# A two-layer diffusion trunk: the first layer's two projections change places, and every projection takes its jobs one token tile at a time

## The reference

```python
h_l = modulate(x, norm1_g[layer], sh1, sc1)      # rmsnorm(x, g) * (1 + scale) + shift
# even layer: one projection h @ ev_w_in, 2304 columns, cut into
#   qa 512, ka 512, va 512 (differential attention), qb 512, kb 128, vb 128 (windowed attention)
qa = rmsnorm(qa.reshape(B, N, DIFF_HEADS, 2, HEAD_DIM), q_g)     # ka, qb, kb likewise
if rope:                                          # latent tokens only
    qa, ka, qb, kb = [rope_2d(t, cos, sin) for t in (qa, ka, qb, kb)]
# odd layer: h @ od_w_in = q_a 512, kv_a 256, k_r 32, nq 512, nk 512, nv 512
```

## Time and profile before

| | us |
|---|---|
| median of 3 runs (3949.11 to 3957.30) | 3950.14 |
| the profiled execution's own time | 3954.3 |
| its span | 3952.5 |
| PE busy in it | 3590.1 (91%) |
| VectorE busy | 2003.9 (51%) |
| ScalarE busy | 1296.8 (33%) |
| GpSimd busy | 171.2 (4%) |

### The profile page before, as it was taken

How to read it: one execution, slowest core, us unless ns; L and a number is a source line. 1 busy time by engine, 2 the same in 40 slices (tenths; PEclk the granted TensorE clock), 3 DMA queues, 4 the chain that set the end, 5 groups by cost and what they waited for, 6 DMA issues and landing times. The chain is left out here.

```text
span 3952.5 us, 47916 instructions
## 1 busy us (share of the span) xinstructions
PE 3590.1 (91%) x17932; PEld 2879.1 (73%) x17932; DVE 2003.9 (51%) x2906; ACT 1296.8 (33%) x2312; POOL 171.2 (4%) x186
## 2 busy tenths in 40 slices
PE   8687889696899999999997979699799889999999
PEld 2476766586788888888885858577577688888887
DVE  2474355586664444434454445588654373333333
ACT  2353234465441111111114535466433351111111
POOL 0210020000120000000001100000000020000000
PEclk9898989898999999999998989799899999999999
DMA  8345464441332222212213344422444331111112
GB/s 309 102 150 174 127 134 97 98 107 59 94 89 65 65 69 60 60 54 68 68 43 133 133 160 136 120 67 58 95 90 106 97 104 46 45 49 48 50 53 69
DMA packets 439684, 370.72 MB, mean 94 GB/s; under 512 B 103509, under 2 KB 382437, under 8 KB 434405
## 3 DMA queue, kind: packets, MB, share of 16 engines
q1 hardware_dynamic: 439525, 368.61, 32.8%
HBM read 280.86 MB, written 87.69 MB: 93 GB/s over the span
## 5 line engine op out<-in xcount | busy, mean ns | idle before, releaser
L2036 DVE SCALAR_TENSOR_TENSOR xT<-ps,mods,xT 128x1024 f32<-128x1024 f32 x192 | 189.4, 1014 | 424.0 <-PE ps L2250 424.0
L2250 PE MATMUL ps<-e_gh,e_w2h 128*128 128x512 f32 x1280 | 356.8, 377 | 5.9 <-DVE e_w2l L2492 3.6
L2250 PE MATMUL ps<-e_gl,e_w2h 128*128 128x512 f32 x1280 | 352.8, 373 | 0.0
L2250 PE MATMUL ps<-e_gh,e_w2l 128*128 128x512 f32 x1280 | 352.3, 373 | 0.0
L2542 DVE TENSOR_TENSOR e_plain<-e_plain 128x1280 f32<-128x1280 f32 (+1 forms) x64 | 86.9, 1358 | 479.6 <-ACT e_plain L2407 479.6
L2250 PE MATMUL ps<-e_hl,e_w1h 128*128 128x512 f32 (+1 forms) x1200 | 327.2, 370 | 0.0
L2250 PE MATMUL ps<-e_hh,e_w1l 128*128 128x512 f32 (+1 forms) x1200 | 327.2, 370 | 0.0
L2250 PE MATMUL ps<-e_hh,e_w1h 128*128 128x512 f32 (+1 forms) x1200 | 327.1, 370 | 0.0
L2407 ACT ACTIVATE e_plain<-ps 128x1280 f32<-128x1280 f32 (+1 forms) x64 | 72.7, 1135 | 758.5 <-PE ps L2250 757.0
L2250 PEld LDWEIGHTS ps<-e_gh,e_w2h 128*128 128x128 f32 x1280 | 225.0, 190 | 55.3 <-DVE e_gl L2546 8.0
L2250 PEld LDWEIGHTS ps<-e_gh,e_w2l 128*128 128x128 f32 x1280 | 226.3, 190 | 43.5
(11 more groups left out here) (349 smaller groups left out, 7458.8 us busy)
## 6 DMA issues: line engine op xcount, KB each, us to landing
e_raw<-in_mlp_w SPq DMA_DIRECT2D x64, 512.0 KB, 4.2
e_raw<-in_mlp_w SPq DMA_DIRECT2D x128, 256.0 KB, 3.0
aw<-in_ada_w SPq DMA_DIRECT2D x12, 2048.0 KB, 8.2
e_raw<-in_w_out SPq DMA_DIRECT2D x48, 512.0 KB, 3.8
rstd<-in_ada_w SPq DMA_DIRECT2D x64, 384.0 KB, 3.4
qkC<-pc_stage SPq DMA_DIRECT2D x72, 192.0 KB, 2.7
hT<-pa_hb SPq DMA_DIRECT2D x10, 1024.0 KB, 5.4
qkA<-pa_stage SPq DMA_DIRECT2D x20, 512.0 KB, 3.2
```

The lines of the kernel that those rows point to most:

```text
L2036: ins = k.nc.vector.scalar_tensor_tensor(out=x, in0=ps, scalar=k.mods[:, layer, gate, bass.ds(n, 1), w], in1=x, op0=ALU.mult, op1=ALU.add)
L2250: mm = pe.matmul(k.ps[:, SB * (e % 2) + b, 0:n], w[:, e % 2, f], m[:, f, c0:c0 + n], start=(f == 0 and x == 0), stop=(f == nf - 1 and x == 2))
```

## The change

The list of jobs goes through all units of a tile before the next tile, from tile 0 on; before, tiles 0 and 1 went through each unit together. With that `split_at` is the first job of the tile, always, and is dropped. And `pb` is called first, with `keeps_h=True`, and `pa` second, with `keeps_h=False`.

```diff
-    jobs = [(t, j) for j in range(U) for t in range(2)] + [(t, j) for t in range(2, NT) for j in range(U) if t < LT or not units[j].latents]
+    jobs = [(t, j) for t in range(NT) for j in range(U) if t < LT or not units[j].latents]
...
-    split_at = [first_of[0]] + [max(first_of[t], last_of[t - 1] + 1) for t in range(1, NT)]
...
-                    for x in range(NT - 1):
-                        if keeps_h and n == split_at[x]:
-                            modulate(x + 1, range(KT // 2, KT))
+                    if keeps_h and n == first_of[t] and t + 1 < NT:
+                        modulate(t + 1, range(KT // 2, KT))
...
-                    for x in range(NT - 1):
-                        if keeps_h and n == split_at[x]:
-                            split_h(x + 1)
-                            inverse(x + 2)
+                    if keeps_h and n == first_of[t] and t + 1 < NT:
+                        split_h(t + 1)
+                        inverse(t + 2)
...
-        project(k, "pa", 0, ev, 0, 1024, [
-            Unit(0, 512, 8, ins["diff_q_g"][0], HD ** -0.5, True, k.qkA, 0),
-            Unit(512, 512, 8, ins["diff_k_g"][0], 1.0, True, k.qkA, 8)], keeps_h=True)
         project(k, "pb", 0, ev, 1024, 1280, [
             Unit(512, 512, 8, ins["swa_q_g"][0], HD ** -0.5, True, k.qkB, 0),
             Unit(1024, 256, 2, ins["swa_k_g"][0], 1.0, True, k.qkB, 8, v=128, v_dst=k.vB),
-            Unit(0, 512, v=512, v_dst=k.vA)], keeps_h=False)
+            Unit(0, 512, v=512, v_dst=k.vA)], keeps_h=True)
+        project(k, "pa", 0, ev, 0, 1024, [
+            Unit(0, 512, 8, ins["diff_q_g"][0], HD ** -0.5, True, k.qkA, 0),
+            Unit(512, 512, 8, ins["diff_k_g"][0], 1.0, True, k.qkA, 8)], keeps_h=False)
```

## The result

| | before | changed |
|---|---|---|
| median, us | 3952.11 (4 runs, 3949.11 to 3957.30) | 3917.39 (4 runs, 3915.37 to 3924.55) |
| profiled execution's own time | 3954.3 | 3915.37 |
| its span | 3952.5 | 3913.6 |

The ratio is 0.991 with a 95% interval of 0.9895 to 0.9926: 29 to 41 us less. A second set of runs gave 0.9905 (0.9891 to 0.9919). Forecast were 3907 and a range of 3899 to 3922. The median of 3917 lies inside that range, but outside the narrower 3901 to 3914 that the forecast gave for itself: a drop of 43 us was forecast, and 35 and 37 came.

A forecast was written before the change was run, and what follows sets the result against it. TensorE, busy 91% of the span, was taken as the bound, with time to win only where it stands still. 10.8 + 0.5 + 20.5 + 11.4 = 43.2 us off a median of 3950.14 gave 3907, 8-in-10 range 3899 to 3922.

The forecast's parts named there:

- Steady tiles of `pa`: `pa` after its third tile: input fetched from memory two tiles ahead ends the stalls, 10.8 us won, bounds 0 and 10.8.
- The chain of 7.65 us: `pa`, end of first job to ready input: transposes 0.84, second job 5.53, idle 1.28; taken as the same in `pb`.
- Steady tiles of `pb`: `pb` after its third tile, now building `h`: no stall, 118.8 us as today; bounds 0 and a 12 us loss.
- The cover of 9.4 us: `pb`, the rest of a tile behind its first job, 14.95 - 5.54, said to exceed the 7.65 us to the next input.
- Rival 1: The tile build stalls `pb`, VectorE instructions stretching when POOL builds a tile: price 12 us, 3919 us, chance 11%.
- First pass of `pa` second: `pa` up to its third tile: 32.2 us instead of 52.7, 20.5 us won, bounds 18 and 22.5.
- First pass of `pb` first: `pb` up to its third tile: 48.7 us against 49.3 today, 0.5 us won, bounds -4 and +7.
- The odd stage: `pd`: job (0,1) fills the wait and third-unit casts start earlier, 11.4 us won, bounds 0 and 14.
- rival 2: The odd stage wins nothing because its last slices are bound by transfers: price 11.4 us, 3918.5 us, chance 11%.
- rival 3: All passes over the weights end late, costing 7 us in `pb`, 2.5 in `pa`, 12 in `pd`: 3929 us, chance 6%.
- rival 5: The changed order does not shorten the stages since something else gates their end: 3950 us, chance 4%.
- rival 4: Slower than before: in `pb` the chain from first job to next input outlasts the tile; 61 us, 3968 us, chance 2%.

The follow-up runs named there:

- the exchange alone: The kernel before with only the calls swapped, `pb` first building `h` and `pa` second, old job list kept: 3937.45 us, ratio 0.9966.
- late tile 2: The changed kernel with GpSimd's build of tile 2 held back until VectorE has cut the last weight slice: 3909.65 us, ratio 0.9888.
- the build behind the last job: The changed kernel with the next tile's second modulation half, cast and split queued behind a tile's last job instead of its first: 4011.13 us.
- build before heads: The kernel before with the next tile's second modulation half and cast ahead of the job's norm, and split ahead of its heads: 3965.26 us, ratio 1.0027.
- tile 1 before the tables: The late tile 2 kernel with GpSimd's build of tile 1 also moved ahead of its rotation tables: 3911.94 us, ratio 0.9894 against the kernel before.

## Why the prediction was right, and where it was not

- Steady tiles of `pa`, 10.8 us: 10.6, in this kernel and with the exchange alone. The number was right and the reason given for the stall was not. The chain of 7.65 us left out the transposes ahead of the second job; from the end of a tile's first job to the next tile it is 8.6 us, and it is no chain but part of a loop through heads, GpSimd's contention and ScalarE's order. Of the 10.6 us the loop is 8.0; the other 2.6 are the cold start behind the wait before tile 2, which the forecast counted here without naming it. The gain came out right because it was taken from the measured stretch and not from the chain.
- Steady tiles of `pb`: no stall, as said. The cover of 9.4 us held, but for a chain of 6.1 us and not the 7.65 of the forecast, so with 3.3 us to spare instead of 1.7. The forecast took the chain over from `pa`, where it was no chain: the verdict was right and its margin was not reasoned. Rival 1 is out for the steady tiles.
- First pass of `pa` second: 20.3 of 20.5, job (0,1) ending at 19.5 us as worked out. First pass of `pb` first: 0.5 us lost instead of won. Job (0,2) began 0.8 us earlier than forecast (24.7 us behind the first matmul, against 25.5) and took 9.3 us instead of 7.3 without its transposes, with the same late second slice as in the odd stage below.
- The odd stage: 9.3 instead of 11.4. The step that was off is the cost of job (0,2), 7.3 us of products with a cold start: it took 10.6 with its transposes less 0.84, 9.7. Its casts ended at 2085.2, 0.9 us later than I had them behind the first matmul, and its second slice came 2.8 us after the first, behind GpSimd's build of tile 2. Some 1.3 of the 2.4 us are that wait and the rest is that thirteen matmuls and not nine came at the slower pace. That is the mechanism which I had priced as rival 1, in another place: I moved cuts beside a build and did not look at what GpSimd does then. The kernel with the late tile 2 shows it: there the products take 7.3 us and nine matmuls are slow, as forecast, and what is left of the difference is 0.58 us of PE waiting for the transposes' input.
- Rivals 2, 3 and 5 did not come; of rival 4 the build behind the last job shows the mechanism, at 48.6 us in `pb` (217.3 against 168.7) when nothing covers it.
- In the first pass the list decides more than the exchange does. In the first passes of `pa` and `pb` together the list is worth 15 us on the kernel before and 16 on top of the exchange, the exchange about 4 (3.6 and 4.5); in the odd stage the list is worth 9.3.

## What to carry to other kernels

Before setting a chain of waits against its cover, follow it once round. If its last instruction releases what its first one waits for, or stands just ahead of it in the same queue, as here, it is a loop. Then the loop's length against the round of the engine that should be the limit decides, and moving one member forward can make it longer. When an order moves work of one engine, look at what the other engines run beside it at the new place, GpSimd beside VectorE above all. And take the size of a gain from a measured stretch; that stands even when the story about its cause falls.

## What the runs showed of the hardware

A float32 VectorE instruction of 128x512 with two inputs in SBUF, 0.68 us alone, took up to 2.91 us when a GpSimd multiplication of 2.3 to 2.9 us was already running. In the traces of four kernels (before, changed, build before heads, tile 1 before the tables) each such instruction that was stretched ended 0.54 or 0.55 us behind the GpSimd instruction, whether it had begun 1.44 us behind that one's start (193.88, kernel before, 1.50 us long) or 0.04 us behind it (the row below, beside a build from 151.46 to 153.84). So it waits until the GpSimd instruction has ended, and its length says when it began. Which of the two waits can turn on the order in which they begin: in the steady tiles of the changed kernel's `pb` the low part starts 0.03 us behind the build and keeps its 0.68 us, and there it is the build that is longer, 2.96 us against 2.34 with nothing beside it (at 214.63 and 133.35).

VectorE's timeline in the kernel with tile 1 ahead of the tables:

```profile
151.49 2.89 DVE L657 TENSOR_TENSOR pb_qh<-pb_yh,pb_qh 128x512 fp32r<-128x512 f32 x1
```

A reduction with a single input kept its 0.69 us beside such a build (L669 at 220.97, kernel before).

TensorE's matmuls of 512 columns came 0.43 us apart instead of 0.23 behind each idle of 3.71 us and more before them in the rows shown, at once or after two or three matmuls. Where it was measured, behind the last job's build, such a wait cost 1.8 us beyond itself. Behind the idles of 1.0 and 1.3 us in steady tiles the pace stayed at 0.23 us after the first matmul (0.50 us long), and the wait cost 0.2 us beyond itself (16.17 - 14.95 - 1.01, and 14.23 - 12.74 - 1.28).
